# The gates of a group of 16 expert blocks: twelve transfers of 256 KB, or one of 3 MB

## The reference

```python
def peer_ffn(h, w_query, sub_keys, expert_u, expert_v):
    ...
        cand_s = cand_s.reshape(b, t, PEER_HEADS, PEER_TOPK * PEER_TOPK)
        cand_i = cand_i.reshape(b, t, PEER_HEADS, PEER_TOPK * PEER_TOPK)
        best_s, pos = lax.top_k(cand_s, PEER_TOPK)
        expert_idx = jnp.take_along_axis(cand_i, pos, axis=-1)
        gate = jax.nn.softmax(best_s, axis=-1)
        u = expert_u[expert_idx]
        v = expert_v[expert_idx]
        act = jax.nn.gelu(jnp.einsum('btd,bthkd->bthk', x_blk, u).astype(jnp.float32), approximate=False)
        return jnp.einsum('bthk,bthkd->btd', (gate * act).astype(v.dtype), v)
```

## Time and profile before

| what | value |
|---|---|
| median of 3 runs | 2193.31 us (2183.31 to 2201.32) |
| profiled execution, own time | 2197.78 us |
| its span, first to last instruction | 2196.5 us |
| PE / DVE / ACT / POOL busy | 2017.2 / 1398.3 / 935.8 / 610.4 us |
| mean granted TensorE clock | 0.948 of full speed |
| DMA traffic, mean | 432.39 MB, 197 GB/s |

### The profile page before, as it was taken

One profiled execution on the slowest core, in us unless ns is written; L12 is line 12 of the kernel. 1 busy time (PEld: TensorE's weight loads), 2 busy tenths in 40 slices (PEclk: granted clock), 3 DMA queues, 4 the chain that ended last, 5 costly groups with the idle time before them and its releaser, 6 DMA issues.

```text
span 2196.5 us, 29043 instructions
## 1 busy us (share of the span) xinstructions
PE 2017.2 (92%) x11145; PEld 1795.6 (82%) x11145; DVE 1398.3 (64%) x2493; ACT 935.8 (43%) x1601; POOL 610.4 (28%) x462
## 2 busy tenths in 40 slices
PE   7898899999999999999977588998999898999998
PEld 6797767888999999999867577787777687898788
DVE  2667755212999999998676676776667685001351
ACT  6633375322334766758622133333333334323243
POOL 3566421241001111032355322222222221443003
PEclk9999999999999999999998899999999999999599
DMA  5221001322556777779999988998998884221001
GB/s 187 97 97 58 20 1 39 126 77 88 172 170 220 244 257 257 249 280 309 316 339 330 384 297 314 307 312 301 315 314 297 306 296 163 96 97 58 0 38 50
DMA packets 150218, 432.39 MB, mean 197 GB/s; under 512 B 14016, under 2 KB 73408, under 8 KB 140608
## 3 DMA queue, kind: packets, MB, share of 16 engines
q1 hardware_dynamic: 94784, 271.12, 35.6%
q0 software_dynamic: 36864, 134.23, 18.0%
q10 hardware_dynamic: 18432, 25.17, 3.2%
HBM read 378.04 MB, written 52.43 MB: 196 GB/s over the span
## 4 chain that ended last, share of the span: by engine, by line
PE 59%; DVE 15%; DMA 10%; ACT 3%; issue 2%; POOL 1%; SPq 1%; ACTq 0%; DVEq 0%
PE PS L700 21%; PE PS L662 9%; PE PS L406 7%; PE PS L398 6%; DMA UG<-in_u_rows,IDX 6%; DMA WR<-in_v 4%; DVE WS L1569 3%; PE PS L678 2%; DVE UG L1552 2%; PE PS L727 2%; PE PS L750 2%; PE PS L441 1%; PE PS L438 1%; DVE OJ L1583 1%; DVE OA L1583 1%
## 5 line engine op out<-in xcount | busy, mean ns | idle before, releaser
L662 PE MATMUL PS<-HS,WS 128*128 128x384 f32 x3072 | 567.0, 343 | 51.9 <-DVE WS L1569 51.2
L700 PE MATMUL PS<-WS,WH 128*128 128x512 f32 x2304 | 558.1, 404 | 51.1 <-DVE WH L1704 51.1
L662 PEld LDWEIGHTS PS<-HS,WS 128*128 128x128 f32 x3072 | 546.1, 193 | 58.0 <-issue 51.2
L700 PEld LDWEIGHTS PS<-WS,WH 128*128 128x128 f32 x2304 | 445.0, 194 | 164.1 <-DVE WH L1704 42.0
L1846 POOL DMA_INDIRECT UG<-in_u_rows,IDX x128 | 168.6, 1317 | 549.6 <-DVE OWN L1552 374.1
L1794 POOL TENSOR_TENSOR WS<-WR,WS 128x1024 fp32r<-128x1024 f32 x94 | 225.3, 2419 | 291.6 <-ACT WS L809 291.6
L1710 DVE TENSOR_TENSOR WS<-WR,WS 128x1024 fp32r<-128x1024 f32 x128 | 156.7, 1225 | 164.4 <-ACT WS L1109 157.7
L1846 POOL DMA_INDIRECT UG<-in_v,IDX x128 | 130.0, 1015 | 457.4 <-DVE X L1560 447.3
L398 PE MATMUL PS<-HS,WS 128*128 128x512 f32 x960 | 225.1, 394 | 0.0
L406 PE MATMUL PS<-WS,HS 128*128 128x256 f32 x1728 | 211.2, 285 | 9.9 <-DVE HSM L1232 9.9
L406 PEld LDWEIGHTS PS<-WS,HS 128*128 128x128 f32 x1728 | 210.0, 194 | 10.5 <-DVE HSM L1232 10.3
(11 more groups left out here) (239 smaller groups left out, 2192.5 us busy)
## 6 DMA issues: line engine op xcount, KB each, us to landing
WR<-in_u SPq DMA_DIRECT2D x128, 512.0 KB
WR<-in_v SPq DMA_DIRECT2D x128, 512.0 KB
WR<-in_w_in SPq DMA_DIRECT2D x27, 1024.0 KB, 4.9
activations<-GA ACTq DMA_DIRECT2D x128, 192.0 KB
gates<-SC SPq DMA_DIRECT2D x24, 1024.0 KB
GB<-gates SPq DMA_DIRECT2D x8, 3072.0 KB, 17.4
GA<-activations SPq DMA_DIRECT2D x128, 192.0 KB, 2.5
WR<-in_w_out SPq DMA_DIRECT2D x8, 1024.0 KB, 5.7
```

The costliest lines, as they stand in the source:

```text
L662: ins = te.matmul(ps[:, 0:DENSE], m.UH[:, (e + 2) % NS, w, k, :], m.HS[:, h, k, 512 - DENSE:512], start=k == 0 and n == 0, stop=k == 7 and ...
L700: ins = te.matmul(ps[:, :], m.WH[:, i % NW, w, tt * 128:tt * 128 + 128], m.VH[:, (i + 2) % NS, v, dh * 512:dh * 512 + 512], start=i == 0 a ...
```

## The change

A group's gates are loaded in twelve DMAs, each of two of the 24 sets (256 KB). For group 0 the twelve stand one behind the other where the one stood. For group g + 1 they stand one behind each `fetch_v` of the blocks 4 to 15 of group g; the blocks 0 to 3 of a group have none behind them. `gated` waits for all twelve of its group: 16 x 12 in place of 16. The runs of 1 KB, the bytes and the halves of `GB` stay as they are.

```diff
--- before.py
+++ after.py
@@ -1695,7 +1695,7 @@
     def gated(i):
         g = i // GRP
         dv.wait_ge(s.back[i % NA], 16 * (i // NA + 1))
-        dv.wait_ge(s.g_in[g % 2], 16 * (g // 2 + 1))
+        dv.wait_ge(s.g_in[g % 2], 16 * (TB // 2) * (g // 2 + 1))
         ga = m.GA[:, i % NA, :].rearrange("p (b t) -> p b t", b=TB)
         ve.tensor_tensor(ga, ga, m.GB[:, g % 2, :, i % GRP, :], ALU.mult).then_inc(s.gated, 1)
 
@@ -1935,13 +1935,15 @@
         dm.wait_ge(*G.free("gate", tb * PER + PER - 1))
         sp.dma_start(m.GD[tb], m.STG[tb % 2]).then_inc(s.g_out[tb % 2], 16)
 
-    def gates_in(g):
+    def gates_in(g, n):
+
         if g < 2:
             dm.wait_ge(s.g_out[0], 16 * TB // 2)
             dm.wait_ge(s.g_out[1], 16 * TB // 2)
         else:
             dm.wait_ge(s.gated, GRP * (g - 1))
-        sp.dma_start(m.GB[:, g % 2].rearrange("p b i t -> p b (i t)"), m.GD[:, :, g * GRP:g * GRP + GRP, :].rearrange(
+        b = slice(2 * n, 2 * n + 2)
+        sp.dma_start(m.GB[:, g % 2, b].rearrange("p b i t -> p b (i t)"), m.GD[b, :, g * GRP:g * GRP + GRP, :].rearrange(
             "b p i t -> p b (i t)")).then_inc(s.g_in[g % 2], 16)
 
     def bring(i):
@@ -1958,16 +1960,16 @@
         for tb in range(TB):
             if HOT_AT[tb * PER + PER - 1] + NS + 1 == e:
                 gates_out(tb)
-    gates_in(0)
+    for n in range(TB // 2):
+        gates_in(0, n)
     for i in range(NA):
         fetch_v(i)
         bring(i)
-    gates_in(1)
     for i in range(NA, 128):
-        if i % GRP == NA and 1 <= i // GRP < NG - 1:
-            gates_in(i // GRP + 1)
         bring(i)
         fetch_v(i)
+        if i % GRP >= NA and (i - NA) // GRP + 1 < NG:
+            gates_in((i - NA) // GRP + 1, i % GRP - NA)
     fetch(B_IN2)
     fetch(B_IN2 + 1)
```

## The result

The changed kernel takes 2125.61 us (2121.59 to 2163.71, 4 runs), the kernel before beside it 2188.31 us (2176.57 to 2201.32, 4 runs). The ratio is 0.9694, 95% interval 0.965 to 0.9739: 3.1% faster. A second comparison, with 6 runs of the changed kernel and 17 of the one before, gave 0.9716 (0.9679 to 0.9752). The ratios leave out runs some 40 us above the others, such as the one of 2163.71 us. The forecast was 2140 with a range of 2128 to 2167.

What follows compares the result with a forecast made beforehand. In the expert stage PE sets the pace between holes where v waits behind 3 MB of gates. 38.98 + 17.5 - 3.5 = 53 us off 2197.8, then 4.5 less for the runs' median, gives 2140 us (2128 to 2167).

Steps and rivals of the forecast that it cites:

- The holes, 38.98 us: Seven idle stretches of PE in line 700's expert stage, v waiting behind 3 MB of gates; all 38.98 us come back.
- The clock, 17.5 us: PE's slower running after each hole in the expert stage would go with the holes, giving 17.5 us.
- Issues and group 0, zero: SP's extra issues, 4.7 us for group 0's twelve, fit in SP's idle time: cost zero, range 0 to 5.
- Late v, 3.5 us: v weights landing later in blocks with a piece cost 0.5 us a group, 3.5 in all, bounds 0 and 35.
- rival A: v lands late in every block that carries a piece, costing 16 to 35 us: 2153 to 2172 us, chance 0.15.
- the loop: From v issue over split and low half to v issue three blocks on: landing L allows (L + 4.9) / 3 us a block.
- the 3.9 us of lead: DVE's low half in the expert stage is ready 3.9 us before PE wants it, so some lateness is covered.
- The share of 1.06: DMA engine share worked out for blocks with a piece, equal to the backlog's, so hardly any room.
- B: The holes stay because a group's bytes, not their burst, are the limit: 2193 us, chance 0.06.
- C: Each small transfer occupies the DMA queue for its fixed part, 6.4 us a block: 2325 us, chance 0.04.
- the last of the sum: From the profiled execution's forecast of 2144.8 us, 4.5 us were taken off to reach the runs' median: 2140.3.

Runs made afterwards that it cites:

- the pieces twice: Changed kernel with each piece of groups 1 to 7 loaded once more, SP waiting for the copy before; median 2178.61 us, ratio to kernel before 0.9963.
- the filling: Score matmuls of the windowed attention's second unit issued twice: changed kernel 2112.49 us (median, second time), kernel before 2165.01 us.

## Why the prediction was wrong in size and right in kind

*The holes, 38.98 us.* Right: all gone, and the two runs with the burst elsewhere show why. Twelve pieces in a row bring them back; the whole transfer in ACT's queue doesn't. v's place behind 3 MB in SP's queue is the cause.

*The clock, 17.5 us.* Right. 539.95 us are 128 blocks at 4.2 and 2.4 more, the slow start of the stage (3.0 foreseen).

*Issues and group 0, zero.* The cost is right: a GA issue is 0.32 us, and from the first issue of the gates to PE's first matmul of line 700 are 44.5 to 47.0 us in the seven profiles with twelve pieces for group 0, 44.7 to 47.4 in the four with one transfer. The working is not: the twelve issues took SP 15.89 us, not 4.7. It cost nothing because before SP stood as long at the v issue behind the gates, which ended 20.7 us after the gates were asked for; now it ends after 16.5. That the stage began 4.2 us later isn't the pieces' doing: the first issue of the gates itself came 6.4 us later, behind code that is the same in both kernels. PE's first matmul of line 700 comes at 1247.04 to 1251.32 us in the four profiles, at 1248.66 to 1255.52 in the seven.

*Late v, 3.5 us.* Mis-sized at both ends. The landing was put at 6.4 us; where it is waited for it is 7.8 at the median, so rival A was half right: v is late in most blocks with a piece (53 splits wait), and by the loop even L = 8.0 gives 4.3 us a block. But 0.1 x 12 = 1.2 us of slip a group is well inside the 3.9 us of lead. It cost nothing. The share of 1.06 that I worked out came as 0.99 to 1.00.

*Rivals.* A's mechanism appears, v late in most blocks with a piece, but without a price. The run with doubled bytes doesn't give it one, since SP's added wait may have cost the 50 us. B is excluded by the timeline. C, a fixed time of each transfer that holds the queue, would show with twelve pieces against three of 1 MB: line 700 takes 540.0 and 542.0 us, so small transfers cost nothing here. On this point the Trainium skill ("DMA: Bandwidth & Descriptors", section Bandwidth) advises 1 MiB or more for each DMA; these two runs show no gain from it in this stage. The 2.0 us per transfer that the prediction takes from the Trainium skill's section "Anatomy of one DMA" on the same page stand there for DMAs that GpSimd issues; the pieces are issued by SP, and no run here shows that figure for them.

*The step that failed* is the last of the sum: "the median of the runs is 4.5 us below it: 2140.3". I took the profiled execution for a typical one and the 18 us between the runs for scatter around it. It was one of the long ones, with 348.1 us behind the stage, while the changed kernel nearly always has 329. The half clock stood in the trace of before: 0.50 for 65 us, with a hole of 1.67 us ahead of it. Since all gate transfers belong to the expert stage, I had "looked at nothing else".

The result lies 14.7 us below 2140.3. Of these 4.1 come from the stage, where 53.0 us were foreseen and 57.1 came (3.5 of the 4.1 are the late v). The other 10.6 come from the base: 2193.31 - 57.1 is 2136.2, still inside the range. A sum from the lower group, whose profile came later with 2173.29 us, gives 2173.3 - 53 = 2120, and a range around that would have held the time.

*What stays open.* Why the stretch lasts 24, 65 or, in the profile of the pieces twice, 109 us, and why the kernel before has the middle length often, twelve in a row never in ten runs and the changed kernel never in eleven. With three pieces of 1 MB the profile has it. With the filling the clock doesn't fall there; what decides when it returns no run shows. How many more bytes the stage could take is open too.

## What to carry to other kernels

A large transfer that isn't urgent belongs in a queue where nothing urgent stands behind it, or cut up between the urgent ones; how finely matters little (256 KB and 1 MB do the same here) as long as the consumer's lead covers one piece. Check the bytes per block first: a demand of 359 GB/s, worked out from the bytes, fitted under PE's pace; what more would have fitted no run here shows. Where the runs of a kernel fall into groups, find out which group the profiled one belongs to and look for a stretch at half clock before its span is taken for the base of a sum; a hole of 1.67 us with small matmuls behind it cost 11 to 52 us here (the part behind the stage took 329.0 to 369.4 us, and 317.7 with the hole filled), and filling it cost nothing that could be measured.

## What the runs showed of the hardware that I had not expected

- SP's issues take long once about 3 MB are asked for on its queue, whatever the size of the DMAs: behind one of 3 MB the next issue took 7.54 us, and twelve issues of 256 KB take 15.89 us at the end of the first stage and 8.59 us at a hole, where one of 256 KB in the middle of a group takes 0.43.
- A burst of 3 MB in a queue of its own beside a busy one takes 31.7 us to land, not 17.4, and lets the other queue's transfers through: ACT waited at most 4.4 us for v, where it waited up to 11.7 behind the burst.
- A hole of 1.67 us on PE ahead of small matmuls went with 24 to 109 us at half clock in nine profiles, with PE busy by its records; with the hole at 0.37 or 0.38 us there was none in three profiles, and the times of 18 runs fit that.
